# VectorE's order in the first attention: two caps move between the weights of a pair of parts

## The reference

```python
z = jnp.einsum("bhqd,bhkd->bhqk", q_blk, kf) * scale          # 8 heads of 64
mask = k_pos[None, :] < q_pos[:, None]
log_not = jnp.where(mask, jax.nn.log_sigmoid(-z), 0.0)
suffix = lax.cumsum(log_not, axis=3, reverse=True) - log_not
weights = jnp.where(mask, jnp.exp(jax.nn.log_sigmoid(z) + suffix), 0.0)
out = jnp.einsum("bhqk,bhkd->bhqd", weights, vf)
```

## Time and profile before

| | |
|---|---|
| median of 3 runs | 3831.64 us (3829.66 to 3836.98) |
| the profiled execution | 3835.95 us, span 3834.2 us |
| TensorE busy | 3614.7 us (94%) |
| VectorE busy | 2192.6 us (57%) |
| ScalarE busy | 977.4 us (25%) |
| GpSimd busy | 392.4 us (10%) |
| mean granted TensorE clock | 0.971 |

### The profile page before, as it was taken

How to read it: one execution, slowest core, us unless ns; L and a number is a source line. 1 busy time by engine, 2 the same in 40 slices (tenths; PEclk the granted TensorE clock), 3 DMA queues, 4 the chain that set the end, 5 groups by cost and what they waited for, 6 DMA issues and landing times. The chain is left out here.

```text
span 3834.2 us, 43194 instructions
## 1 busy us (share of the span) xinstructions
PE 3614.7 (94%) x17211; PEld 2861.9 (75%) x17211; DVE 2192.6 (57%) x2986; ACT 977.4 (25%) x1986; POOL 392.4 (10%) x174
## 2 busy tenths in 40 slices
PE   7997889999998999977799999999999999989989
PEld 6663677888887778866678888887777777765687
DVE  6677376565557465999574444447333334355493
ACT  1566230000003251134240000004113223232462
POOL 0114022322231001313000000000000000000000
PEclk9998999999999999998899999999999999999899
DMA  4100222222222021120121111113111221333022
GB/s 164 34 23 23 77 97 81 81 81 81 103 97 98 27 91 45 43 75 3 42 85 45 44 44 44 66 44 124 63 53 61 80 80 56 126 119 131 18 67 77
DMA packets 137390, 267.61 MB, mean 70 GB/s; under 512 B 11680, under 2 KB 42516, under 8 KB 137236
## 3 DMA queue, kind: packets, MB, share of 16 engines
q1 hardware_dynamic: 137236, 265.50, 19.5%
HBM read 220.39 MB, written 45.09 MB: 69 GB/s over the span
## 5 line engine op out<-in xcount | busy, mean ns | idle before, releaser
L130 PE MATMUL banks<-region_parts 128*128 128x512 f32 x2650 | 1062.3, 401 | 30.8 <-PEq L3185 6.5
L132 PE MATMUL banks<-region_parts,weight_chunks_parts 128*128 128x512 f32 x2112 | 825.6, 391 | 0.0
L131 PE MATMUL banks<-weight_chunks_parts,region_parts 128*128 128x512 f32 x1984 | 778.0, 392 | 0.0
L132 PE MATMUL banks<-region_parts 128*128 128x512 f32 x1632 | 640.5, 392 | 0.0
L130 PEld LDWEIGHTS banks<-region_parts 128*128 128x128 f32 x2650 | 502.7, 190 | 142.6 <-issue 22.0
L132 PEld LDWEIGHTS banks<-region_parts,weight_chunks_parts 128*128 128x128 f32 x2112 | 397.6, 188 | 84.6
L131 PEld LDWEIGHTS banks<-weight_chunks_parts,region_parts 128*128 128x128 f32 x1984 | 376.8, 190 | 81.0 <-issue 4.4
L131 PE MATMUL banks<-region_parts 128*128 128x512 f32 x1018 | 398.0, 391 | 0.0
L130 PE MATMUL banks<-region_parts,extra_parts 128*128 128x512 f32 x992 | 392.9, 396 | 0.9 <-PEq L1711 0.5
L466 ACT ACTIVATE region<-constants 128x512 f32<-128x512 f32 x128 | 81.1, 634 | 1226.5 <-DVE constants L461 1226.5
L131 PE MATMUL banks<-region_parts,extra_parts 128*128 128x512 f32 x992 | 386.7, 390 | 0.0
(11 more groups left out here) (387 smaller groups left out, 4754.3 us busy)
## 6 DMA issues: line engine op xcount, KB each, us to landing
weight_chunks<-in_w_in SPq DMA_DIRECT2D x19, 2048.0 KB, 8.2
weight_chunks<-in_w_up SPq DMA_DIRECT2D x16, 2048.0 KB, 8.7
weight_chunks<-in_w_down SPq DMA_DIRECT2D x16, 2048.0 KB, 7.8
extra<-in_w_ada SPq DMA_DIRECT2D x16, 1536.0 KB, 11.0
x_spill<-region SPq DMA_DIRECT2D x32, 512.0 KB, 2.6
weight_chunks<-in_w_out SPq DMA_DIRECT2D x8, 2048.0 KB, 8.0
region<-x_spill SPq DMA_DIRECT2D x32, 512.0 KB, 6.1
f_spill<-region SPq DMA_DIRECT2D x64, 256.0 KB, 2.0
```

What stands on the lines that cost most here:

```text
L130: pe.matmul(out, m.parts(lhs[0]), m.parts(rhs[0]), start=first, stop=False)
L131: pe.matmul(out, m.parts(lhs[0]), m.parts(rhs[1]), start=False, stop=False)
L132: return pe.matmul(out, m.parts(lhs[1]), m.parts(rhs[0]), start=False, stop=last)
```

## The change

The second `weights` call of a pair moves behind the two `cap` calls of the next pair. No other engine's order changes, and no instruction is added or taken away.

```diff
             for i in range(NP + 1):
                 if i and i % 2 == 0:
                     weights(i - 2)
-                    weights(i - 1)
                 if i < NP and i % 2 == 0:
                     cap(i)
                     cap(i + 1)
+                if i and i % 2 == 0:
+                    weights(i - 1)
                 if i in split_at:
```

## The result

The changed kernel took 3843.96 us (median of 9 runs, 3840.6 to 3845.97) against 3833.27 us for the kernel before on the same chip (9 runs, 3829.66 to 3836.98): a ratio of 1.0026, 95% interval 1.0018 to 1.0034. It is slower by 10.7 us, outside the predicted range of 3823 to 3841, on the side to which the prediction gave 0.10. The profiled execution after took 3840.60 us, its span 3838.8.

A forecast was written before the change was run, and what follows sets the result against it. TensorE was taken to bound three quarters, the loop between VectorE and ScalarE the fourth. Gains 3.9 + 0.6 = 4.5 less losses 2.8 + 1.0 = 3.8 give 0.7 us less: 3831.64 - 0.7 = 3831, range 3823 to 3841.

The forecast's parts named there:

- So I cost these pairs at nothing: Capped pairs where TensorE is the bound: second weights behind the caps still come in time, cost 0.
- The covers behind it, 0.2 and 1.0 us: Pair at 159.76: second weights end 0.2 us before TensorE's second turn, second sigmoids 1.0 us before the next scores.
- The gain of the fourth quarter, 3.9 us: Fourth quarter: VectorE's waits at five capped pairs (0.57, 0.79, 1.00, 0.57, 1.00) are covered, 3.9 us won.
- The quarter starts, 3.8 us: Starts of quarters two to four: GpSimd holds the second weights' product, 2 x 1.4 plus 1.0 us lost.
- The first quarter, 0.6 us won: First pairs of the first quarter: 0.6 us won, between nothing and the 1.07 us that TensorE waited.
- gains without losses: Rival: fourth and first quarter waits go, second weights slip in ahead of GpSimd; 7.5 us less, 3824; chance 0.09.
- two further pairs: Fourth quarter, in the rival at 3824: waits of two other capped pairs go too, about 0.7 us.
- GpSimd's hold at the starts: Rival at quarter starts: scan and product both held, weights 3.3 us late, clock falls; 8 slower, 3840; chance 0.10.
- the caps' wait over 18 pairs: Rival: weights behind caps end 0.4 us after the turn wants them, 18 pairs cost 7.2 us; 3838; chance 0.06.
- The 0.75 for no change: Whole kernel: gains and losses of 4 us each, no measurable change, range 3826 to 3837; chance 0.75.
- the turns at the starts: At 172, 243 and 312 us TensorE's turn waits 1 to 2 us for a product that GpSimd held.
- its 2 us: First three quarters: TensorE stays as busy, each quarter within 2 us of its length.

The follow-up runs named there:

- takes-only run: New order only at the seven take steps (12, 28, 36, 52, 60, 76, 84), all else as in the kernel before: 3835.22 us, ratio 1.0009.
- the run with the old order at the takes: The changed kernel with the old order at the seven steps where ScalarE does a take: 3837.74 us, ratio 1.0014.
- step 74 alone: New order at step 74 only, all else as in the kernel before: 3832.53 us, ratio 0.9999.
- rest-only run: New order at the 21 places that are neither take steps nor quarter starts, all else as in the kernel before: 3832.51 us, ratio 1.0000.
- 74 and 76 only: New order at steps 74 and 76 only, all else as in the kernel before: 3837.34 us, ratio 1.0010.
- first three only: New order in the first three quarters only (steps below 72), all else as in the kernel before: 3841.66 us, ratio 1.0020.
- take moved ahead: The changed kernel with ScalarE's take put between the first and second sigmoids of its step: 3835.59 us, ratio 1.0008.
- old at 76: The changed kernel with the old order at step 76 alone: 3839.99 us, ratio 1.0020.
- old at 74: The changed kernel with the old order at step 74 alone: 3841.17 us, ratio 1.0014.

## Why the prediction was wrong

**What bounds the kernel** was read rightly: TensorE in three quarters, the loop of VectorE and ScalarE in the fourth. That VectorE's 62.2 us of waits were not the kernel's time was right as well. 29.5 us of them are gone and the kernel is longer.

**The step that failed** is "So I cost these pairs at nothing". The covers behind it, 0.2 and 1.0 us, were right for the pair on which they were worked out (0.29 and 1.06 after). They were carried to all capped pairs, and at seven take steps the work behind the second sigmoids is not the next scores alone but copy, take, head sums and then the scores, with no cover (0.11 us at step 52 before). The prediction named the place as a thing that would make it wrong (ScalarE's copies behind its second sigmoids) and did not work it out. It costs 3.2 us in the first three quarters by the takes-only run, 3.8 by the run with the old order at the takes, and cutting the link there leaves nothing of it. At the other capped pairs "nothing" was nearly right: the rest only loses 1.0 us over these quarters, and through which pairs was not followed.

**The gain of the fourth quarter, 3.9 us**, was a sum of waits, each taken as won, and place by place it was right: step 74 alone wins 0.7 (0.57 in the sum), step 76 in the takes-only run 1.0 (0.79), step 84 there 0.8 (0.57), and the rest-only run less step 74 another 1.6 (1.00 + 1.00 at steps 78 and 92): 4.1 together. In the whole change the quarter became 3.8 us longer. The step that failed here is the adding up: the prediction let no pair affect the next. Steps 74 and 76 each win by themselves and together lose 3.4: the second weights held at step 74 make TensorE's second turn and the scores of 76 late, so the second weights there start behind waiting caps and beside GpSimd's work, with sigmoids, take and head sums behind them. By parts the fourth quarter comes to 1.55 (start) + 3.4 (74 and 76) - 0.8 (step 84, takes only) - 1.6 (the rest's 2.3 less the 0.7 of step 74) = 2.6 of the 3.8 measured. By the lags most of the remaining 1.2 us arises at step 78, right behind the pile-up: from pair 38 to 39 the lag falls by 2.19 us in the rest-only run and by 1.39 with step 74 alone, so the new order at 78 wins 0.8 there; behind a new step 76 it falls by 0.91 in the changed kernel and by 1.07 with 74 and 76 only, so it wins nothing. That TensorE's low clock adds to the loss is read from the rows and was not tested by itself, and GpSimd's splits of `mixT` and `w_out`, which hold the second weights at step 76, were not left out in any run.

**The quarter starts, 3.8 us**: mechanism and size were right, 4.1 measured alone in one execution (1.55, 1.07, 1.55 for 1.4, 1.4, 1.0), and the part of it in TensorE's bound goes away without the moving averages. The product was held at every start, the scan not in the changed kernel, but in four of the others at the third quarter's start (3.02 us for 1.28). The Trainium skill (SBUF — State Buffer, the part on the shared port pair) lets such an instruction of VectorE and one of GpSimd exclude one another, whichever starts first running whole. That the two exclude one another and that a scan can be held agrees with the traces; the order doesn't show in them, as in the four cases the scan was held although its record starts 0.04 to 0.05 us ahead of GpSimd's.

**The first quarter, 0.6 us won**: wrong in sign. The turn's wait of 1.07 us did not go (1.17 at 118.15 after). The lag dips to -0.79 at pair 2 and is 1.16 at the quarter's end, of which the take at step 12 has 1.0 by the takes-only run.

**The rivals.** The first, gains without losses, had 0.7 us for two further pairs, which is read low: they wait 0.59 us (312.99) and 0.74 (343.26); its 3824 hardly moves. The slower case was given 0.10 for GpSimd's hold at the starts at 3840, and 0.06 for the caps' wait over 18 pairs. The first mechanism is 4 of the 10.3 us, and the clock did not fall at the two starts in TensorE's bound. The second names the right wait (caps for scores) with the wrong path behind it: not the second turn late by 0.4 us at 18 pairs, but the take behind the second sigmoids, about 0.6 us at each of five, and a pile-up at step 76. The 0.75 for no change rested on the cost at nothing and on gains that add up.

**What was to be seen.** VectorE's waits for sigmoids fell to 32.7 us (about 40 predicted) and its waits at L3517 grew to 48.1; the turns at the starts waited 1.22, 1.23 and 2.38 us (1 to 2 predicted, so the last is above it). The second quarter stayed within its 2 us (1.9), the third did not (3.9), and the fourth came out 3.8 us longer for 2 to 4 shorter.

**Open**: why the third quarter's start takes 2.1 us more in some kernels (in the profiled executions of four: first three only, take moved ahead, old at 76, old at 74), though the scan starts equally long ahead of GpSimd. Each kernel was traced in one execution, so this may differ between executions of one kernel as well. Open too are the shares of the low clock and of GpSimd's splits in the loss at steps 74 to 78, and what the earlier take gives the old order.

## What to carry to other kernels

When an instruction is put behind one that waits, follow everything behind it round the whole circle of engines back to itself, and do so for each kind of iteration: the rare one with an extra step (here a take every 8 to 16 parts) is where the cover is missing. A long wait of an engine off the critical path isn't a gain to be had, and gains worked out at single places don't add up when each place delays the input of the next. Where a rare step must not be late, it can be moved ahead of the work that became late: here this did as much as taking the order back at its steps (292.9 us for 293.9).

## What the runs showed of the hardware

Of two instructions that started 0.04 to 0.05 us apart on VectorE and GpSimd, one took its own time and the other nearly the time of both (1.27 + 1.89 = 3.16 us): the scan 1.27 us and GpSimd's 2.91 (247.54 in the changed kernel), or GpSimd's 1.89 and the scan 3.02 (247.39 with the first three quarters changed). Which way it went differed between single executions of kernels whose instructions at that place are identical, and was worth 2.1 us of lag.

Leaving out GpSimd's moving averages made the order of before 9.0 us faster by the medians (3832.36 less 3823.39), nearly as much as the whole change took, though VectorE's waits in the attention hardly differ (62.6 us for the sigmoids without them, 62.2 with). A held instruction counts as busy: VectorE is busy for 210.03 us of the attention with the averages and for 189.49 without, with the same instructions. A hold shows only as a duration beside that of the same form elsewhere.
